# State space heads: decay rows by transfers within SBUF in place of TensorE, and products in pairs on two halves of the output partitions

## The reference

```python
def ssd_chunked_scan(xs, dt, a, bm, cm):
    log_a = (dt * a)...                       # per head, per position
    xdt = (xs * dt[..., None])...
    a_cum = jnp.cumsum(log_a, axis=-1)
    seg = a_cum[..., :, None] - a_cum[..., None, :]
    decay = jnp.where(tril, jnp.exp(jnp.where(tril, seg, 0.0)), 0.0)
    cb = jnp.einsum('bclgn,bcsgn->bgcls', cc, bc)
    y_diag = jnp.einsum('bgrcls,bcsgrp->bclgrp', cb[:, :, None] * decay, xdt)
    ...                                       # states carried from chunk to chunk
    return (y_diag + y_off).reshape(b, s, g, r, p)
```

## Time and profile before

| | us |
|---|---|
| median of 3 runs | 1643.34 (1631.63 to 1649.98) |
| profiled execution, its own time | 1646.69 |
| its span in the trace | 1645.0 |
| TensorE busy in the span | 1597.3 (97%) |
| VectorE busy | 1159.6 (70%) |
| ScalarE busy | 807.7 (49%) |

### The profile page before, as it was taken

The page is one execution under the profiler, slowest core; times in us unless marked ns, Lnnn a source line. Parts: engine busy times, 40 slices in busy tenths (PEclk is TensorE's granted clock), DMA queues, the critical chain, the costliest instruction groups (busy, mean ns, idle before and its releaser), DMA issues.

```text
span 1645.0 us, 33704 instructions
## 1 busy us (share of the span) xinstructions
PE 1597.3 (97%) x13254; PEld 1567.6 (95%) x13254; DVE 1159.6 (70%) x1357; ACT 807.7 (49%) x973; POOL 26.3 (2%) x53
## 2 busy tenths in 40 slices
PE   7999999999999999999999999999799999999997
PEld 7998899989999999999999999999799999999996
DVE  6676677765678988888888888667664544664755
ACT  6444355544554545545545455444454544454542
POOL 0000000000000000000000000000000000000000
PEclk9999999999999999999999999999899999999999
DMA  9353344455548777787777875555455555455451
GB/s 347 137 180 129 128 153 142 154 184 185 184 160 335 271 271 297 258 303 274 258 290 270 302 288 188 189 187 183 141 188 185 189 184 168 139 170 174 156 180 52
DMA packets 85187, 336.17 MB, mean 204 GB/s; under 512 B 9456, under 2 KB 9712, under 8 KB 78704
## 3 DMA queue, kind: packets, MB, share of 16 engines
q1 hardware_dynamic: 77328, 281.05, 49.5%
q0 software_dynamic: 7056, 51.38, 8.5%
q10 hardware_dynamic: 720, 2.52, 0.4%
HBM read 332.82 MB, written 2.10 MB: 204 GB/s over the span
## 4 chain that ended last, share of the span: by engine, by line
PE 72%; DVE 5%; issue 2%; ACT 1%; DVEq 0%; ACTq 0%
PE PS L1097 23%; PE PS L1101 23%; PE PS L1099 23%; DVE ada_w L932 1%; DVE wlo L587 1%; ACT whi L255 1%; PE PS L1198 1%; DVE UV L890 1%; PE PS L1165 1%; PE PS L1343 0%; DVE X L1084 0%; PE PS L1184 0%; DVE rb L621 0%; DVE X L603 0%; PE PS L1144 0%
## 5 line engine op out<-in xcount | busy, mean ns | idle before, releaser
L1097 PE MATMUL PS<-gh,whi 128*128 128x256 f32 x3520 | 998.9, 284 | 14.6 <-DVE wlo L587 9.6
L1099 PE MATMUL PS<-gl,whi 128*128 128x256 f32 x3520 | 984.5, 280 | 0.0
L1101 PE MATMUL PS<-gh,wlo 128*128 128x256 f32 x3520 | 984.3, 280 | 0.0
L587 DVE TENSOR_TENSOR wlo<-raw,whi 128x1024 fp32r<-128x1024 f32 x528 | 644.7, 1224 | 421.1 <-ACT whi L255 420.0
L255 ACT ACTIVATE whi<-raw 128x1024 fp32r<-128x1024 f32 x528 | 557.7, 1060 | 718.5 <-PE PS L1101 716.1
L1097 PEld LDWEIGHTS PS<-gh,whi 128*128 128x128 f32 x3520 | 665.8, 189 | 21.9 <-issue 20.6
L1099 PEld LDWEIGHTS PS<-gl,whi 128*128 128x128 f32 x3520 | 667.2, 190 | 2.8 <-issue 1.9
L1101 PEld LDWEIGHTS PS<-gh,wlo 128*128 128x128 f32 x3520 | 667.4, 190 | 0.0
L1097 PE MATMUL PS<-ah,whi 128*128 128x256 f32 x704 | 198.8, 282 | 10.8 <-DVE UV L890 7.2
L1099 PE MATMUL PS<-al,whi 128*128 128x256 f32 x704 | 197.3, 280 | 0.0
L1101 PE MATMUL PS<-ah,wlo 128*128 128x256 f32 x704 | 197.3, 280 | 0.0
(11 more groups left out here) (187 smaller groups left out, 793.9 us busy)
## 6 DMA issues: line engine op xcount, KB each, us to landing
raw<-weights SPq DMA_DIRECT2D x528, 512.0 KB, 3.4
ada_w<-w_ada POOLq DMA_DIRECT2D x48, 1024.0 KB, 5.2
outT<-X SPq DMA_DIRECT2D x4, 512.0 KB, 2.6
X<-xT SPq DMA_DIRECT2D x3, 512.0 KB, 8.7
c<-const ACTq DMA_DIRECT2D x1, 1536.0 KB, 6.3
c_act<-c_rows POOLq DMA_DIRECT2D x1, 1024.0 KB, 9.0
X<-xT SPq DMA_DIRECT2D x2, 256.0 KB, 5.0
prm<-params ACTq DMA_DIRECT2D x1, 276.5 KB, 4.3
```

Source lines behind the costliest of these rows:

```text
L587: dve.tensor_tensor(wlo[:, j % SPLIT, :], raw[:, j, :], whi[:, j % SPLIT, :].bitcast(F32), ALU.subtract).then_inc(s_lo, 1)
L1097: pe.matmul(out[:, t, :], whi[:, b, w], hi[:, kt, :], start=first and half == 0 and t % 2 == 0, stop=False, skip_group_check=True)
L1099: pe.matmul(out[:, t, :], whi[:, b, w], lo[:, kt, :], start=False, stop=False, skip_group_check=True)
L1101: mm = pe.matmul(out[:, t, :], wlo[:, b, w], hi[:, kt, :], start=False, stop=last and half == 1, skip_group_check=True)
```

## The change

1. The 16 products that spread the decay rows (line 1257) go. ScalarE writes the 16 rows, with the second half twice, to a new tile `ACUM` of 16 partitions by 3 x 128 (two copies at n = 19). GpSimd's queue then issues 16 transfers within SBUF: transfer h reads the one partition h of `ACUM` (1,536 bytes) for each of the 128 partitions and writes `EM[:, h]`.
2. `EM` has a buffer for every head (24 KB per partition) and lies where `ada_w` and `c_act` are put later. So the transfer of `c_act` goes behind the 16 and behind the wait for slot 87, and its silu from n = 32 to n = 115.
3. VectorE's `decay` reads and writes `EM` in place. Before head 0 it waits until all 16 transfers have landed (`s_r` at 256).
4. The exponential and the product with C·B take two heads in one instruction, in the odd slots, and the products with dt·x of two heads go together: both first products, even head and odd head, then both second ones.

```diff
@@ gpsimd
-            pool.wait_ge(s_gh, DT)
+            pool.wait_ge(s_at, 2)
+            for h in range(SSM_HEADS):
+                pool.dma_start(EM[:, h, :, :].rearrange("p k l -> p (k l)"),
+                               ACUM[h:h + 1, :, :].rearrange("p k l -> p (k l)").unsqueeze(1).to_broadcast([1, P, 3 * P])).then_inc(s_r, 16)
+            pool.wait_ge(s_evac, G_OUT + 2)
             pool.dma_start(c_act[:, :], c_rows).then_inc(s_crow, 16)
-            pool.wait_ge(s_evac, G_OUT + 2)
@@ scalar
-                    act.activation(small[0:16, 256:512], PS[0:16, 7, S:2 * S], ACT.Copy).then_inc(s_at, 1)
-                if n == 32:
+                    act.activation(ACUM[:, 0:2, :], PS[0:16, 7, S:2 * S].rearrange("p (k l) -> p k l", k=2), ACT.Copy
+                                   ).then_inc(s_at, 1)
+                    act.activation(ACUM[:, 2, :], PS[0:16, 7, S + P:2 * S], ACT.Copy).then_inc(s_at, 1)
+                if n == IN_SLOTS + 27:
                     act.wait_ge(s_crow, 16)
                     act.activation(c_act[:, :], c_act[:, :], ACT.Silu).then_inc(s_c, 1)
-                if 35 <= n < 35 + SSM_HEADS:
-                    h = n - 35
-                    act.wait_ge(s_e, 3 * h + 3)
-                    act.activation(EM[:, h % 3, :, :], EM[:, h % 3, :, :], ACT.Exp).then_inc(s_ex, 1)
+                if 35 <= n < 35 + SSM_HEADS and n % 2:
+                    j = (n - 35) // 2
+                    act.wait_ge(s_e, 6 * j + 6)
+                    act.activation(EM[:, 2 * j:2 * j + 2, :, :], EM[:, 2 * j:2 * j + 2, :, :], ACT.Exp).then_inc(s_ex, 1)
@@ vector
             def decay(h):
-                dve.wait_ge(s_r, h + 1)
                 if h == 0:
+                    dve.wait_ge(s_r, 16 * SSM_HEADS)
                     dve.wait_ge(s_nb, 1)
-                if h >= 3:
-                    dve.wait_ge(s_y, h - 2)
                 for k in range(3):
-                    lo = P if k else 0
-                    dve.tensor_scalar(EM[:, h % 3, k, :], PS[:, 4 + h % 2, lo:lo + P], NB[:, k, h:h + 1], 0.0,
-                                      ALU.add, ALU.min).then_inc(s_e, 1)
+                    dve.tensor_scalar(EM[:, h, k, :], EM[:, h, k, :], NB[:, k, h:h + 1], 0.0, ALU.add, ALU.min
+                                      ).then_inc(s_e, 1)
...
@@ tensor
-                if 34 <= n < 34 + SSM_HEADS:
-                    h = n - 34
-                    pe.wait_ge(s_xd, 16)
-                    if h >= 2:
-                        pe.wait_ge(s_e, 3 * h - 3)
-                    pe.matmul(PS[:, 4 + h % 2, 0:S], ident[0:16, h:h + 1].to_broadcast([16, P]), small[0:16, 256:512],
-                              start=True, stop=True).then_inc(s_r, 1)
-                if 37 <= n < 37 + SSM_HEADS:
...
+                if 37 <= n < 37 + SSM_HEADS and n % 2:
+                    j = (n - 37) // 2
+                    pe.wait_ge(s_m, j + 1)
+                    if j >= 2:
+                        pe.wait_ge(s_yo, 2 * (j - 2) + 1)
+                    for c in range(2):
+                        for q in (2 * j, 2 * j + 1):
+                            lo = 64 * (q % 2)
+                            out = PS[lo:lo + 64, 6 + j % 2, P * c:S]
+                            em = EM[:, q, 0:2, :] if c == 0 else EM[:, q, 2, :]
+                            mm = pe.matmul(out, XD[:, c, 64 * q:64 * q + 64], em, start=(c == 0), stop=(c == 1),
+                                           skip_group_check=True)
+                    mm.then_inc(s_y, 1)
```

More of the change, by code:

```diff
@@ L126, in build @@
         assert o <= nc.sbuf_usable_end, (o, nc.sbuf_usable_end)
+        EM, e = place("EM", [P, SSM_HEADS, 3, P], offset=ada_at)
+        assert e <= area
+        ACUM, _ = place("ACUM", [SSM_HEADS, 3, P], offset=area + 1024 * Q0)
         SQX1, _ = place("SQX1", [P, 2, 4, S], offset=area + 1024 * Q0)
@@ L133, in build @@
         XD, o = place("XD", [P, 2, D // 2], offset=late)
-        EM, o = place("EM", [P, 3, 3, P], offset=o)
         CB, o = place("CB", [P, 2, 3, P], offset=o)
@@ L724, in decay, with weigh @@
             def decay(h):
-                dve.wait_ge(s_r, h + 1)
                 if h == 0:
+                    dve.wait_ge(s_r, 16 * SSM_HEADS)
                     dve.wait_ge(s_nb, 1)
-                if h >= 3:
-                    dve.wait_ge(s_y, h - 2)
                 for k in range(3):
-                    lo = P if k else 0
-                    dve.tensor_scalar(EM[:, h % 3, k, :], PS[:, 4 + h % 2, lo:lo + P], NB[:, k, h:h + 1], 0.0,
-                                      ALU.add, ALU.min).then_inc(s_e, 1)
-            def weigh(h):
-                dve.wait_ge(s_ex, h + 1)
-                if h == 0:
+                    dve.tensor_scalar(EM[:, h, k, :], EM[:, h, k, :], NB[:, k, h:h + 1], 0.0, ALU.add, ALU.min
+                                      ).then_inc(s_e, 1)
+            def weigh(j):
+                dve.wait_ge(s_ex, j + 1)
+                if j == 0:
                     dve.wait_ge(s_cbm, 4)
-                dve.tensor_tensor(EM[:, h % 3, :, :], EM[:, h % 3, :, :], CB[:, h // 8, :, :], ALU.mult).then_inc(s_m, 1)
+                pair = EM[:, 2 * j:2 * j + 2, :, :]
+                dve.tensor_tensor(pair, pair, CB[:, j // 4, :, :].unsqueeze(1).to_broadcast([P, 2, 3, P]), ALU.mult
+                                  ).then_inc(s_m, 1)
             def ssm_out(j):
-                dve.wait_ge(s_y, 2 * j + 2)
+                dve.wait_ge(s_y, j + 1)
                 dve.wait_ge(s_z, 1 + j // 4)
@@ L845, in slot1 @@
                     decay(n - 34)
-                if 35 <= n < 35 + SSM_HEADS:
-                    weigh(n - 35)
+                if 35 <= n < 35 + SSM_HEADS and n % 2:
+                    weigh((n - 35) // 2)
                 if 38 <= n < 54 and n % 2 == 0:
@@ L1251, in slot1 @@
                     pe.matmul(PS[:, 6 + g, S:S + P], bm[:, P:S], cm[:, P:S], start=True, stop=True).then_inc(s_cb, 1)
-                if 34 <= n < 34 + SSM_HEADS:
-                    h = n - 34
-                    pe.wait_ge(s_xd, 16)
-                    if h >= 2:
-                        pe.wait_ge(s_e, 3 * h - 3)
-                    pe.matmul(PS[:, 4 + h % 2, 0:S], ident[0:16, h:h + 1].to_broadcast([16, P]), small[0:16, 256:512],
-                              start=True, stop=True).then_inc(s_r, 1)
-                if 37 <= n < 37 + SSM_HEADS:
-                    q = n - 37
-                    lo, bank = 64 * (q % 2), 6 + q // 2 % 2
-                    pe.wait_ge(s_m, q + 1)
-                    if q >= 4:
-                        pe.wait_ge(s_yo, 2 * (q // 2 - 2) + 1)
-                    pe.matmul(PS[lo:lo + 64, bank, 0:S], XD[:, 0, 64 * q:64 * q + 64], EM[:, q % 3, 0:2, :],
-                              start=True, stop=False, skip_group_check=True)
-                    pe.matmul(PS[lo:lo + 64, bank, P:S], XD[:, 1, 64 * q:64 * q + 64], EM[:, q % 3, 2, :],
-                              start=False, stop=True, skip_group_check=True).then_inc(s_y, 1)
+                if 37 <= n < 37 + SSM_HEADS and n % 2:
[11 more added lines that the diff above has]
+                    mm.then_inc(s_y, 1)
                 if n in (55, 56):
```

## The result

The changed kernel takes 1682.51 us (median of 4 runs, 1671.30 to 1685.72) against 1646.39 us for the one before (4 runs): the ratio is 1.022, with a 95% interval of 1.018 to 1.026. It is slower by 36 us. The profiled execution took 1685.72 us.

The account below looks back on a forecast made before the run. TensorE, busy 97% of the span, was taken as the bound. A 79.3 us later first pair, less 8.5 (spreading products) and 5.0 (pairs), plus 2.0 (clock), gave +67.8 us on the 1643.34 us median: 1711 us, range 1622 to 1740.

Parts of the forecast that it names:

- the likeliest case: Transfers within SBUF: one source partition as slow as one lane, 1711 us, own range 1695 to 1740; chance 0.58.
- the hidden case: Transfers finish within the 44 us free, needing over 72 GB/s from one partition: 1627 us, 1622 to 1630; chance 0.28.
- The spreading products, 11.8 us: TensorE's head slots: removal saves 0.85 us in 3 slots and 0.71 us in 13, 11.8 us in all.
- The pairs, 5.0 us: TensorE's products of two heads: 8 pairs save 5.0 us, the middle of 1.8 and 8.2 us.
- The cover of the pairs' work, of the silu and of the load: VectorE and ScalarE: idle time covers these; VectorE at worst takes back 2.4 us, load and silu cost 0, at most 1.
- The transfers, 126 us: Sixteen transfers from single partitions at one lane's best rate, 24.9 GB/s: 126 us, landed at 212.1 us.
- case in between: Source gives 40 to 72 GB/s, or single lanes serve several transfers at once: 1630 to 1665 us; chance 0.08.
- Where it stops: Slot 34: VectorE waits at decay(0) for the last transfer, TensorE after unit 37; first products start 79.3 us later.
- worse: the weights are starved as well: DMA lanes: weights stand wholly behind the transfers, TensorE runs out near unit 28, 1739 us and more; chance 0.06.
- the prediction's own signs: Profile after: TensorE waits some 80 us before slot 37's products, VectorE waits before its first decay, among others.
- The clock, +2.0 us: TensorE after the stall: granted clock falls, 4 us at the lower level (1.2 GHz), 2 us lost.
- The 44 us: Time free for the transfers between their issue and VectorE's wait at slot 34, less a transfer's fixed part.

Follow-up runs that it names:

- the pairs alone: Kernel before with two heads' products issued together and EM a ring of eight heads, spreading products kept on TensorE: 1633.32 us against 1640.76 us, ratio 0.995.
- experiment 7: Changed kernel with the 16 transfers issued in the head order 0, 4, 8, 12, 1, 5 and so on: 1626.73 us (one run; 1639.66 us before).
- experiments 8 and 9: Changed kernel with each row on 4 source partitions, next to each other or 8 apart: 1621.9 and 1618.6 us (one run each; 1641 us before).
- the transfers alone: Kernel before with the 16 transfers added to a spare tile nobody reads, c_act's load and silu moved: 1691.21 us, ratio 1.030.
- spread sources: Changed kernel with each row made 16 times by TensorE and each transfer reading 16 source partitions: 1619.54 us against 1640.8 us, ratio 0.988.

## Why the prediction was right, and by how much it was off

It forecast slower by a single slow source, and slower it is: 36 us where 68 were forecast, inside the range of 1622 to 1740 us but below the likeliest case's own range of 1695 to 1740. 1682.5 us lies in no case's own range; the whole range holds it only because it was stretched down to the hidden case. The direction was earned, the size was partly luck. Step by step:

- **The spreading products, 11.8 us:** nearly right. From slot 37's products to those of slot 51 the kernel before takes 199.18 - 138.71 = 60.5 us, the changed one 233.16 - 186.93 = 46.2 us, which is 14.2 us less, where 12 spreading products at 0.71 us and seven pairs at 1.02 us come to 15.7. The two terms together are about a tenth too high.
- **The pairs, 5.0 us:** too low. "Only the passes at the seams can meet" was wrong; two heads take 0.80 us, so the term belongs at the upper end of 8.2 us, or about 7 as measured with the pairs alone. The sentence of the Trainium skill on independent tiles (page "TensorEngine Tiling (Array Packing)", section "Key Properties") is what the trace shows here.
- **The cover of the pairs' work, of the silu and of the load:** right. VectorE waits 8.2 us in all for the eight exponentials (the longest 1.8), and TensorE 1.9 us in all for `EM`, at most 1.4 us once, before the first pair.
- **The transfers, 126 us:** the mechanism was right and the term mis-sized. They took 92.2 us, 34 GB/s in the mean against the 24.9 taken from one lane. While all lanes were on one partition it gave 27 to 29 GB/s, near the forecast; the rest is that lanes ran ahead into transfers from other groups, which the prediction named only in its case in between. The last landed at 176.8 and not 212.1 us. It landed 35 us before its forecast, where the forecast for the time was 32 us too long (67.8 against 36.1, the latter from the medians). The estimate from the Trainium skill ("SBUF — State Buffer", "Door 1: The DMA port swizzle"), 116 us, was nearer and still 24 us too long. Its 27 GB/s per port agrees with the 26 and 29 GB/s that the packets show for one group and for one partition. Its rule that four neighbours share one port fits experiment 7 and the first packets of experiments 8 and 9.
- **Where it stops:** this step failed. The prediction had VectorE wait for `s_r` at slot 34, and set starved weights down as "no cost", on the ground that 16 units would pass in turns. It took a transfer as 128 packets of 1,536 B, each 1 us on its lane; the trace has 48 with data, mostly of 4,608 B, and 2.57 us each at first. Nor were there turns at first: no weight packet between 90 and 100 us, 0.16 MB (16 GB/s) between 100 and 110 us, 1.35 MB (2.6 units) from 90 to 143 us. ScalarE waited 64.2 us for `raw` from slot 28's split on. This is the rival "worse: the weights are starved as well", which had a chance of 0.06 and 1739 us and more; its mechanism came, and its price didn't, since the transfers ended earlier and some units passed in their second half. Two of the prediction's own signs failed with the step: TensorE waited 1.4 us and not some 80 before the first pair, and VectorE did not wait for the transfers before its first `decay`. By luck it made little odds to the sum, since both stalls end when the transfers do: splits follow each other again from 175.97 us on, and `decay(0)` starts at 182.61. Had the wait on `s_r` been taken out as a cure, nothing would have been gained: the transfers alone, without it, cost 53 us.
- **The clock, +2.0 us:** there is no such term behind the first pair. The granted clock was 0.50 (1.2 GHz) between 143 and 150 us, when TensorE had stood still for 33 us, and 1.00 (2.4 GHz) again between 184 and 187 us; what it cost is part of the first pair's delay.
- **The sum, with measured terms:** the first pair at 186.93 against the first head's products at 138.71 is +48.2. Less the 14.2 us gained from there to slot 51, and less 1.0 for slot 52's products, it is +33.0, against +32.9 at the marker. With the prediction's terms of 8.5 and 8.2 it would be +31.5. The first pair came 31 us before its forecast of 218.0: the landing 35 us earlier, and 10.1 in place of 5.9 us from there to the pair, because splits up to that of unit 38 (VectorE, 181.47 us) had still to come before `decay(0)`.
- **The rival "hidden",** 1627 us: its condition was that the source give 72 GB/s. With the heads in another order it gives 69, the transfers land at 129.3 us, and VectorE doesn't wait for them. That the time is then 1626.7 us is chance: it is one run, 12.9 us below the kernel before beside it, where the rival has 16.8, and the weights are still starved (18.0 us of waits for `raw`, marker -9.6 against -17.2 with spread sources). Where the source is really wide, the gain is 21 us. The 44 us were right for VectorE's wait and say nothing of the weights.

## What to carry to other kernels

In these runs a broadcast within SBUF from one partition was a slow transfer on all 16 lanes (27 to 34 GB/s), and its price was paid by the weights on the same lanes: ask first how many bytes come out of one source group, then what else is queued. Spread the source over many partitions, go through HBM, or at least put transfers with distant sources next to each other in the queue. When the lanes' busy share rises while the GB/s fall, look for such a source, and don't look only at the engine that waits for the transfer itself. And here two heads' products of 64 output columns on the two halves cost as much as one head's (0.80 against 0.79 us) when they were issued next to each other.

## What the runs showed of the hardware that I had not expected

- One source partition gave 16 lanes 29 GB/s by its packets (2.57 us for 4,608 B with 16 in flight), four neighbours with four lanes together 26 GB/s, and the order of the same 16 transfers made it 34 or 69 GB/s in the mean.
- 16 transfers in GpSimd's queue let almost no weights pass (43 GB/s in all between 100 and 110 us); the same transfers one by one let 172 GB/s pass at the same busy share of the lanes, most of it in the pauses between two. The share counts lanes that wait for their source as busy.
- ScalarE was held for 62 us in the issue of eight such transfers, while GpSimd issued its eight in 4 us (85.3 to 89.1 us).
- Two heads' products on the two halves overlap whole, 0.80 us for eight passes where four took 0.79 us, although even and odd head alternate in one in-order row.
